# Seven products for the odd layer's key blocks and for the second half of its output projection

## The chip, the core and the metric

The kernel runs on one core of a Trainium2 chip. The metric is the device time of one execution in microseconds (us), as the median of several runs. Durations and waits come from one further execution, taken with the hardware profiler. The engines are PE (TensorE, matmul), DVE (VectorE), ACT (ScalarE), POOL (GpSimd) and SP (SyncE), whose queue issues the weight loads here.

## What is computed

A two-layer trunk on 256 tokens of width 1024, all in float32. Layer 0 mixes tokens by a recurrent branch and sparse attention, layer 1 (the "odd" layer) by retention; after each mixer come a mixture of 32 experts (each token uses 2, every expert's weights are read) and a gated per-layer embedding. The change touches only two products of the odd layer: the key part of `od_w_in` and the projection by `od_w_out`.

```python
def reference(...):
    h = x
    for i in range(DEPTH):                                   # DEPTH = 2
        hn = rms_norm(h, mix_norm_g[i])
        ...
        else:                                                # odd layer
            z = hn @ od_w_in[j]                              # 1024 -> q 1024, k 1024, v 2048, g 2048
            q, k, v, g = _split(z, OD_SPLIT)
            yc = retention_mixer(q..., k..., v..., g, od_gn_g[j])   # 8 heads, rotary q and k
            mix = yc @ od_w_out[j]                           # 2048 -> 1024
        h = h + mix
        h = h + hier_moe(rms_norm(h, ffn_norm_g[i]), ...)    # 32 experts, 1024 -> 512 -> 1024
        e = rms_norm(p[i] @ ple_w_up[i], ple_norm_g[i])
        h = h + e * jax.nn.sigmoid(h @ ple_w_gate[i])
    return h
```

## The kernel before

**Order of the work.** The program is written out by hand, engine by engine; each engine runs its own list in order and semaphores join them. `pe_jobs` lists PE's jobs in order, `banks_of` gives each job one of 8 PSUM banks. `begin` waits until the bank's previous job was emptied, `end` signals "full"; on the other side `full` waits for a job and `emptied`/`taken` free its bank. The tokens' rows are two tiles of 128 (`NT` = 2), `xT` holds the normalised activations turned, features on partitions.

**The odd mixer.** The 1024-wide input meets 12 weight blocks of 1024 x 512 (2 MB each, `rq0`, `rq1`, `rk0`, `rk1`, `rv0..3`, `rg0..3`), then four blocks of the output projection (`rout0..3`, 512 x 1024 each). Query and key blocks go through `tokens` (L629): 8 matmuls of 128x512 for each token tile. DVE then rotates the result (L1774 to L1778), POOL adds the two halves (L1965), PE turns the sum (`turn_rotated`) and ACT copies it out (L1115).

**Seven products.** The four value blocks use the Winograd form of Strassen's scheme. `quarters` cuts a weight block into four quarters of 512 x 256 (B11, B12, B21, B22), `A11..A22` are the quarters of the activations (tile by half of the features). `value_products` (L1038) makes seven products of 4 matmuls of 128x256 (`PRODUCTS`: a, c, b, d, a2, b2, c2) in place of the sixteen matmuls of 128x512. DVE makes the four sums of activations once (`value_sums`, S1 to S4) and four differences of quarters for each block (T3, T1, T2, T4; T1 is written over B12 in the block's slot), one block ahead of PE. ACT copies a, c, b and a2 out, DVE adds the rest together into `rv`.

**The head loop** (`HEAD_STEPS` = 12 steps) runs the 8 heads, the gate blocks and the turned rows `yT0..3`. The output block `rout0` comes in its step 10, `rout1` behind it, then a small product `gain1`, then `rout2` and `rout3`; all go through `held_rows` (L657) into four banks that stay open until `rout3` is done. A 2 MB output block costs 16 matmuls of 128x512. Then DVE adds the banks to `h` (`add_rows`, L1355), with the norm of the first tile in between, and the expert layer `moe(1)` begins: turned rows, routing (L802), the first expert (L874).

**Weights.** Ten slots of 2 MB in `big`: slots 0 to 5 are a ring for the plain blocks; slots 6 to 9 are the `arena`, which holds the mixer's data. SP's queue issues the loads in order and waits before each until its slot is free. For layer 1, experts 0 to 2 take the slots of `EXPERT_SLOTS[1]` in the order gate, up, down: [4, 5, 9], [8, 7, 0], [1, 2, 3]. Slot 9 and those behind it wait for `yT3_1` (`arena_free`), slots 0 to 3 for the reading of `rout0..3`, slot 6 (`SPARE`, a gate of expert 3) for `rout_11`. Half of expert 3's up weights then go into `h` (`lent`) as soon as ACT has copied `h` into PSUM, and later loads wait for an expert to be done.

## Time and profile before

| what | value |
|---|---|
| runs, median (lowest to highest) | 1362.29 us (1360.82 to 1363.45) |
| the profiled execution, its own time | 1363.1 us |
| its span by the trace | 1361.3 us |
| PE busy | 1076.7 us, 79% |
| DVE busy | 355.0 us, 26% |
| DMA queue of the weights | 470.32 MB, 83.7% of 16 engines' span |
| chain that ended last | DMA 48%, PE 46%, DVE 2%, issue 2% |

The busy shares are means over stages with different limits. What counts for a change in one stage is the chain that ended last: for every stretch of time it names the work that the end waited for. A product of a float32 matmul stands in the trace as two records, so 16 matmuls are "x32". The time of an execution is 1.8 us above its span.

### The profile page before, as it was taken

The page shows a single profiled execution, that of the slowest core. Times are in us where ns is not written, and L with a number is a line of the kernel's source. Part 1 is how long each engine was busy: PE and PEld are TensorE (multiplying, and loading weights), DVE is VectorE, ACT ScalarE, POOL GpSimd, SP SyncE. Part 2 cuts the span into 40 slices and gives each one's busy share as a digit, 9 for nine tenths or more (in the row PEclk, how much of TensorE's full clock was granted, in tenths as well). Part 3 has the DMA queues.
Part 4 walks back from the last instruction along what each step waited for, and adds up shares of the span by engine and source line. Part 5 has one row for each costly group of instructions (what it writes and reads, how often), then busy time and mean ns, then how long its engine had stood idle before and what let it go on. Part 6 is the DMA issues. An engine that isn't in the chain of part 4 may idle for free.

```text
span 1361.3 us, 26143 instructions
## 1 busy us (share of the span) xinstructions
PE 1076.7 (79%) x10938; PEld 628.9 (46%) x10938; DVE 355.0 (26%) x826; ACT 170.5 (13%) x411; POOL 90.7 (7%) x226
## 2 busy tenths in 40 slices
PE   6999987676676676689999999988767667766668
PEld 5885554343344343344468554444334333333333
DVE  1596323111111112122254541132211211211121
ACT  2225311000000001001011000121000000000000
POOL 0020011000000000000110100011000000000000
PEclk9999999888888888899999999999888888888889
DMA  9956599999999999998354236789999999999991
GB/s 361 325 197 257 222 403 425 428 430 427 429 429 427 429 428 428 430 407 328 126 183 147 101 124 254 297 345 425 429 428 428 428 428 429 428 428 429 428 416 40
DMA packets 57838, 474.86 MB, mean 349 GB/s; under 512 B 4056, under 2 KB 6104, under 8 KB 32192
## 3 DMA queue, kind: packets, MB, share of 16 engines
q1 hardware_dynamic: 56800, 470.32, 83.7%
q10 hardware_dynamic: 768, 2.57, 0.5%
q0 software_dynamic: 224, 1.31, 0.3%
q8 instruction: 34, 0.56, 0.2%
q14 instruction: 12, 0.10, 0.0%
HBM read 473.12 MB, written 3.16 MB: 350 GB/s over the span
## 4 chain that ended last, share of the span: by engine, by line
DMA 48%; PE 46%; DVE 2%; issue 2%; ACT 1%; SPq 1%; POOL 0%; ACTq 0%; DVEq 0%; POOLq 0%
DMA big<-in_moe_w_up_dram 48%; PE ps L657 10%; PE ps L874 9%; PE ps L629 9%; PE ps L620 5%; PE ps L1038 4%; PE ps L610 1%; PE ps L896 1%; PE ps L785 1%; PE ps L904 1%; SPq L494 1%; PE ps L802 1%; DVE big L1639 0%; DMA h<-in_x_dram 0%; DVE big L1635 0%
## 5 line engine op out<-in xcount | busy, mean ns | idle before, releaser
L874 PE MATMUL ps<-big 128*32 128x256 f32 x4064 | 323.7, 486 | 157.4 <-DMA big<-in_moe_w_up_dram 157.1
L874 PEld LDWEIGHTS ps<-big 128*32 128x32 f32 x4064 | 167.7, 138 | 308.1 <-issue 179.5
L1635 DVE SCALAR_TENSOR_TENSOR big<-big,ps 64x256 f32<-64x256 f32 x64 | 26.4, 413 | 681.3 <-ACT big L1259 681.3
L896 PE MATMUL ps<-big 128*32 128x256 f32 x2048 | 123.8, 382 | 57.7 <-DVE big L1644 57.7
L629 PE MATMUL ps<-big,xT 128*128 128x512 f32 x288 | 125.9, 593 | 2.1 <-DVE xT L1344 1.3
L896 PEld LDWEIGHTS ps<-big 128*32 128x32 f32 x2048 | 59.9, 109 | 108.0 <-DVE big L1644 74.9
L904 PE MATMUL ps<-big 32*128 32x256 f32 x1024 | 73.3, 398 | 41.8 <-ACT big L1270 40.6
L1259 ACT ACTIVATE big<-ps 64x256 f32<-64x256 f32 x64 | 24.1, 377 | 565.9 <-PE ps L874 565.9
L629 PEld LDWEIGHTS ps<-big,xT 128*128 128x128 f32 x288 | 54.3, 190 | 66.2 <-issue 64.3
L904 PEld LDWEIGHTS ps<-big 32*128 32x128 f32 x1024 | 49.5, 184 | 70.8 <-issue 70.8
L657 PE MATMUL ps<-big,xT 128*128 128x512 f32 x160 | 71.8, 607 | 1.5 <-ACT xT L1115 1.5
L620 PE MATMUL ps<-xT,big 128*128 128x256 f32 x320 | 69.9, 380 | 1.5 <-ACT xT L1121 1.5
L1911 POOL TENSOR_TENSOR big<-big,rk 128x64 f32<-128x64 f32 x64 | 18.8, 294 | 773.2 <-PE ps L883 743.8
L657 PE MATMUL ps<-big 128*128 128x512 f32 x160 | 69.5, 593 | 0.0
L844 PE MATMUL ps<-xn,big 128*32 128x256 f32 x1056 | 69.3, 379 | 0.0
L620 PEld LDWEIGHTS ps<-xT,big 128*128 128x128 f32 x320 | 60.6, 190 | 11.7 <-issue 3.7
L657 PEld LDWEIGHTS ps<-big,xT 128*128 128x128 f32 x160 | 30.7, 195 | 39.0 <-issue 36.9
L657 PEld LDWEIGHTS ps<-big 128*128 128x128 f32 x160 | 30.1, 190 | 37.1 <-issue 37.1
L844 PEld LDWEIGHTS ps<-xn,big 128*32 128x32 f32 x1056 | 35.0, 110 | 23.0 <-DVE rk L1597 1.5
L1270 ACT ACTIVATE big<-ps 128x256 f32<-128x256 f32 x64 | 24.5, 383 | 157.0 <-PE ps L896 157.0
L883 PE MATMUL ps<-kept,big 128*32 128x128 f32 x1024 | 40.3, 273 | 0.3 <-issue 0.3
L1639 DVE SCALAR_TENSOR_TENSOR big<-big,ps 64x128 f32<-64x128 f32 x128 | 37.2, 291 | 3.0
(211 smaller groups left out, 805.2 us busy)
## 6 DMA issues: line engine op xcount, KB each, us to landing
big<-in_moe_w_gate_dram SPq DMA_DIRECT2D x64, 2048.0 KB, 33.0
big<-in_moe_w_down_dram SPq DMA_DIRECT2D x62, 2048.0 KB, 38.8
big<-in_moe_w_up_dram SPq DMA_DIRECT2D x60, 2048.0 KB, 37.5
big<-in_od_w_in_dram SPq DMA_DIRECT2D x12, 2048.0 KB, 14.3
big<-in_ev_w_in_dram SPq DMA_DIRECT2D x6, 2048.0 KB, 21.5
big<-in_ple_w_gate_dram SPq DMA_DIRECT2D x8, 1024.0 KB, 20.1
big<-in_od_w_out_dram SPq DMA_DIRECT2D x4, 2048.0 KB, 7.8
big<-in_moe_w_up_dram SPq DMA_DIRECT2D x6, 1024.0 KB, 35.1
```

Of the source, the lines that this page charges most:

```text
L620: ins = nc.tensor.matmul(b[:, i * S:(i + 1) * S], w[:, k, m * P:(m + 1) * P], rhs[:, k, :], start=k == 0, stop=k == KD - 1)
L629: ins = nc.tensor.matmul(b, xT[:, k, t * P:(t + 1) * P], w[:, k, :], start=k == 0, stop=k == KD - 1)
L657: ins = nc.tensor.matmul(banks[job], lhs(k, t), w[:, kk, half * 512:(half + 1) * 512], start=k == 0, stop=k == kt - 1)
L844: ins = nc.tensor.matmul(ps[TOK * q:TOK * q + TOK, 4, 0:QD], pick[:, t, :], xn_t[:, t, q * QD:(q + 1) * QD], start=t == 0, stop=t == NT - 1)
L874: ins = nc.tensor.matmul(ps[TOK * i:TOK * i + TOK, 5, 0:2 * P].rearrange("p (b n) -> p b n", b=2), xe[:, k, :], (low if k < KD // 2 else w ...
L883: ins = nc.tensor.matmul(ps[TOK * q:TOK * q + TOK, 6, t * P:(t + 1) * P], share[:, t, :], ident, start=True, stop=True)
L896: ins = nc.tensor.matmul(ps[TOK * q:TOK * q + TOK, 7, 0:QD], hidT[:, k, :], wd[:, k, q * QD:(q + 1) * QD], start=k == 0, stop=k == KF - 1)
L904: ins = nc.tensor.matmul(ps[:, q, t * QD:(t + 1) * QD], shareT[TOK * q:TOK * q + TOK, t * P:(t + 1) * P], yb[TOK * q:TOK * q + TOK, :], st ...
L1038: ins = nc.tensor.matmul(b, lhs[:, k, :], rhs[:, k, :], start=k == 0 and len(i) == 1, stop=k == HALF - 1, skip_group_check=True)
L1270: sc.activation(yb, ps[:, 7, 0:QD], ACT.Copy).then_inc(y_taken, by)
L1635: ve.scalar_tensor_tensor(out=t2, in0=t2, scalar=1.0, in1=u2, op0=ALU.add, op1=ALU.mult).then_inc(gated_done, by)
L1639: ins = ve.scalar_tensor_tensor(out=hid[2 * TOK * b:2 * TOK * b + 2 * TOK].rearrange("p m k -> p (m k)"), in0=th[0:2 * TOK, b, :], scalar= ...
```

## The change

It turns the two key blocks and the last two output blocks into seven products each.

1. `SEVEN` = rk0, rk1, rv0..3: `products(m)` takes the place of `tokens` for the key blocks and of `value_products`. Six blocks are handled alike, block m in banks 4 to 7 (m even) or 0 to 3 (m odd); `turn_rotated(m + 1)` follows block m for m < 3, in banks 5 and 7 or 1 and 3. DVE now makes the activations' sums and the first block's differences behind the second query tile, ahead of the other two rotations. A key block's results go to `rkraw` in SBUF, and DVE rotates them from there.
2. rout2 and rout3 together are one product of 256 x 1024 by 1024 x 1024, done as seven products of 4 matmuls of 128x512: `last_a`, `last_b`, `last_d`, `last_c` in banks of their own, and three that go on in the banks `rout_00`, `rout_01`, `rout_10`. DVE makes three differences of 128x2048 in step 10 of the head loop and the fourth behind `last_b`, four sums of `yT2` and `yT3` behind the head loop, and adds the parts to `h`.
3. The differences OT2 and OT3 lie in slot 7. So expert 1 gets slots [8, 0, 1] and expert 2 [7, 2, 3], and SP waits for `last_c` and all four differences before slot 7, for `rout_10` before slots 2 and 3, and for `out_parts_used` too before slot 6. `gate1_0` takes slot 7 for slot 1.

```diff
-EXPERT_SLOTS = [[[2, 3, 4], [5, 9, 8], [0, 7, 1]], [[4, 5, 9], [8, 7, 0], [1, 2, 3]]]
+EXPERT_SLOTS = [[[2, 3, 4], [5, 9, 8], [0, 7, 1]], [[4, 5, 9], [8, 0, 1], [7, 2, 3]]]
...
+SEVEN = ("rk0", "rk1", "rv0", "rv1", "rv2", "rv3")
+LAST_BANKS = {"last_b": "yT3_0", "last_d": "yT3_1", "last_c": "gain1"}
...
-    jobs += [f"rv0_{i}" for i in PRODUCTS] + [f"rk1T_{t}" for t in range(NT)]
-    jobs += [f"rv{c}_{i}" for c in range(1, 4) for i in PRODUCTS]
+    jobs += [f"rq0T_{t}" for t in range(NT)]
+    for m, w in enumerate(SEVEN):
+        jobs += [f"{w}_{i}" for i in PRODUCTS] + ([f"{ROTATED[m + 1]}T_{t}" for t in range(NT)] if m < 3 else [])
...
-    jobs += ["gain1"]
+    jobs += ["gain1"] + [f"last_{i}" for i in "abdc"]
...
+                        elif i == RING + 1:
+                            sync.wait_ge(out_tiles_ready, 4)
+                            full(sync, "last_c")
                         expert(l, kind, e, e)
                 if l:
-                    full(sync, "rout_11")
+                    full(sync, "rout_10")
+                    sync.wait_ge(out_parts_used, 1)
...
-            turn_rotated(0)
-            for i, w in enumerate(ROTATED[2:], 1):
-                tokens([f"{w}_{t}" for t in range(NT)], slot(arrived(w), KD, BLK))
-                turn_rotated(i)
...
+            turn_rotated(0)
             pe.wait_ge(sums_ready, 4)
-            value_products(0)
-            turn_rotated(3)
-            for c in range(1, 4):
-                value_products(c)
+            for m in range(len(SEVEN)):
+                products(m)
+                if m < 3:
+                    turn_rotated(m + 1)
...
             gain_rows(1)
-            out_block(2)
-            out_block(3)
...
+            out_product("last_a", OA11, B11)
+            pe.wait_ge(block_read, BLOCK_READ["rout1"])
+            pe.sem_inc(bank_full[BANK["rout_11"]], 1)
+            pe.wait_ge(out_sums_ready, 4)
+            pe.wait_ge(out_tiles_ready, 3)
+            out_product("last_b", OS1, OT1)
+            out_product("last_d", OS2, OT2)
+            out_product("last_c", OS3, OT3)
+            out_product("rout_00", OA12, B21, False)
+            out_product("rout_01", OS4, B22, False)
+            pe.wait_ge(out_tiles_ready, 4)
+            out_product("rout_10", OA22, OT4, False)
             moe(1)
...
+                if m < 2:
+                    for i in ("a2", "b2", "c2"):
+                        taken(dve, f"{w}_{i}")
+                    dve.wait_ge(values_ready, m + 1)
                     for t in range(NT):
+                        rotate(4 + 2 * m + t, rkraw[:, t, :], v)
+                        v.sync()
                         dve.sem_inc(rot_parts, 1)
...
+                if hd == NH + GATE_LAG:
+                    for c in (2, 3):
+                        dve.wait_ge(landed[loads.at[f"rout{c}"]], 16 * loads.turn[f"rout{c}"])
+                    ve.tensor_tensor(OT3, B22, B12, ALU.subtract).then_inc(out_tiles_ready, 1)
+                    ve.tensor_tensor(B12, B12, B11, ALU.subtract).then_inc(out_tiles_ready, 1)
+                    dve.wait_ge(out_tiles_ready, 2)
+                    ve.tensor_tensor(OT2, B22, B12, ALU.subtract).then_inc(out_tiles_ready, 1)
...
+            full(dve, "last_b")
+            ve.tensor_tensor(B12, B21, OT2, ALU.subtract).then_inc(out_tiles_ready, 1)
```

**How the rows stand, at the key blocks.** In the lists below a line number is that of the version shown, "x7" counts matmuls (one record of the list is one matmul, two in the trace), and the semaphores waited for stand in brackets. On PE before, the second key block (bank 1, then 2), the turned key rows (banks 3 and 4) and the first product of `rv0` (bank 4):

```order
L629 MATMUL ps<-big,xT 128x512 [waits bank_free1,landed3]
L629 MATMUL ps<-big,xT 128x512 x7
L629 MATMUL ps<-big,xT 128x512 [waits bank_free2]
L629 MATMUL ps<-big,xT 128x512 x7
L610 MATMUL ps<-kept,big 128x128 [waits bank_free3,rot_ready]
L610 MATMUL ps<-kept,big 128x128 x3
L610 MATMUL ps<-kept,big 128x128 [waits bank_free4,rot_ready]
L610 MATMUL ps<-kept,big 128x128 x3
L1038 MATMUL ps<-big,xT 128x256 [waits bank_free4,landed4,sums_ready]
```

And now, the last three products of the second key block, the turned rows of the first (banks 5 and 7), and the first product of `rv0`:

```order
L1056 MATMUL ps<-big,xT 128x256 [waits bank_free0]
L1056 MATMUL ps<-big,xT 128x256 x3
L1056 MATMUL ps<-big 128x256 [waits bank_free1]
L1056 MATMUL ps<-big 128x256 x3
L1056 MATMUL ps<-big,xT 128x256 [waits tiles_ready,bank_free2]
L1056 MATMUL ps<-big,xT 128x256 x3
L632 MATMUL ps<-kept,big 128x128 [waits bank_free5,rot_ready]
L632 MATMUL ps<-kept,big 128x128 x3
L632 MATMUL ps<-kept,big 128x128 [waits bank_free7,rot_ready]
L632 MATMUL ps<-kept,big 128x128 x3
L1056 MATMUL ps<-big,xT 128x256 [waits bank_free4,landed4]
```

The two runs of 8 matmuls per key block became seven runs of 4 half as wide (four of them stand ahead of the piece), and the bank that `rv0` opens with is no longer one that turned rows have just filled.

On DVE before, from the second difference of `rv0` through the rotation of the second key block to the third difference of `rv1`:

```order
L1748 TENSOR_TENSOR big<-big 128x4x256
L1754 TENSOR_TENSOR big<-big 128x1024 [waits tiles_ready]
L1760 TENSOR_TENSOR big<-big 128x1024 [waits tiles_ready]
L1774 TENSOR_TENSOR xn<-ps,big 128x512 [waits rot_ready,bank_full1]
L1777 TENSOR_TENSOR xn<-ps,big 128x4x64
L1778 TENSOR_TENSOR xn<-ps,big 128x4x64
L1774 TENSOR_TENSOR xn<-ps,big 128x512 [waits bank_free1,rot_ready,bank_full2]
L1777 TENSOR_TENSOR xn<-ps,big 128x4x64
L1778 TENSOR_TENSOR xn<-ps,big 128x4x64
L1743 TENSOR_TENSOR big<-big 128x1024 [waits bank_free2,landed5,bank_full6]
```

And now, from the last additions of `rk0` through its rotation to the first difference of `rv0`:

```order
L1855 TENSOR_TENSOR big<-big,ps 128x256 [waits bank_full6]
L1808 TENSOR_TENSOR big<-big 128x1024 [waits tiles_ready]
L1819 TENSOR_TENSOR xn<-big 128x512 [waits values_ready,bank_free6,rot_ready,bank_free5,bank_free4]
L1821 TENSOR_TENSOR xn<-big 128x4x64
L1822 TENSOR_TENSOR xn<-big 128x4x64
L1819 TENSOR_TENSOR xn<-big 128x512 [waits dve_step,rot_ready]
L1821 TENSOR_TENSOR xn<-big 128x4x64
L1822 TENSOR_TENSOR xn<-big 128x4x64
L1791 TENSOR_TENSOR big<-big 128x1024 [waits dve_step,landed4,bank_full2]
L1796 TENSOR_TENSOR big<-big 128x4x256
```

The rotation of a key block now stands behind the block's last additions and the next block's T4, reads SBUF in place of PSUM, and the differences for the block after next queue behind it.

**At the output projection.** On PE before, `rout1`, `gain1`, `rout2`, `rout3`, and the first turned rows of the expert layer:

```order
L657 MATMUL ps<-big 128x512 x15
L671 MATMUL ps<-xn,kept 32x256 [waits dgain_ready,bank_free1]
L671 MATMUL ps<-xn,kept 32x256 x3
L657 MATMUL ps<-big 128x512 [waits landed2,bank_free2,bank_free0]
L657 MATMUL ps<-big 128x512 x15
L657 MATMUL ps<-big 128x512 [waits landed3,bank_free0,bank_free7]
L657 MATMUL ps<-big 128x512 x15
L610 MATMUL ps<-kept,xn 128x128 [waits xn_ready,landed10,bank_free4,pT_loaded,route_loaded]
L610 MATMUL ps<-kept,xn 128x128 x3
L610 MATMUL ps<-kept,xn 128x128 [waits bank_free6]
```

And now, from `last_a`:

```order
L1118 MATMUL ps<-big 128x512 [waits bank_free6,bank_free5,landed3,landed2,bank_free0]
L1118 MATMUL ps<-big 128x512 x3
L1118 MATMUL ps<-big,xT 128x512 [waits block_read,bank_free5,out_tiles_ready,out_sums_ready]
L1118 MATMUL ps<-big,xT 128x512 x3
L1118 MATMUL ps<-big,xT 128x512 [waits bank_free6]
L1118 MATMUL ps<-big,xT 128x512 x3
L1118 MATMUL ps<-big,xT 128x512 [waits bank_free7]
L1118 MATMUL ps<-big,xT 128x512 x3
L1118 MATMUL ps<-big 128x512 x4
L1118 MATMUL ps<-big,xT 128x512 x4
L1118 MATMUL ps<-big 128x512 [waits out_tiles_ready]
L1118 MATMUL ps<-big 128x512 x3
L632 MATMUL ps<-kept,xn 128x128 [waits xn_ready,landed10,bank_free4,pT_loaded,route_loaded]
```

Two runs of 16 became seven of 4; the first is free to start at once, the second waits for sums and differences from DVE, the seventh for the fourth difference.

On SP before, from expert 0's down weights (slot 9) to those of expert 2 (slot 3), and the gate of expert 3 (slot 6):

```order
L494 DMA big<-in_moe_w_down_dram 128x4096
L494 DMA big<-in_moe_w_gate_dram 128x4096
L494 DMA big<-in_moe_w_up_dram 128x4096
L494 DMA big<-in_moe_w_down_dram 128x4096 [waits block_read]
L494 DMA big<-in_moe_w_gate_dram 128x4096 [waits block_read]
L494 DMA big<-in_moe_w_up_dram 128x4096 [waits block_read]
L494 DMA big<-in_moe_w_down_dram 128x4096 [waits bank_full6]
L548 DMA big<-in_moe_w_gate_dram 128x4096 [waits bank_full6]
```

And now:

```order
L512 DMA big<-in_moe_w_up_dram 128x4096 [waits block_read]
L512 DMA big<-in_moe_w_down_dram 128x4096 [waits block_read]
L512 DMA big<-in_moe_w_gate_dram 128x4096 [waits bank_full7,out_tiles_ready]
L512 DMA big<-in_moe_w_up_dram 128x4096 [waits bank_full3]
L512 DMA big<-in_moe_w_down_dram 128x4096 [waits bank_full3]
L570 DMA big<-in_moe_w_gate_dram 128x4096 [waits out_parts_used,bank_full3]
```

Slots 0 and 1 moved ahead of slot 7; slot 7 now waits for `last_c` and the differences, slots 2 and 3 both for `rout_10`.

## Rows read from the trace of the kernel before

**Rows 1.** the page, the span in 40 slices of 34.03 us
```profile
PEclk9999999888888888899999999999888888888889
GB/s 361 325 197 257 222 403 425 428 430 427 429 429 427 429 428 428 430 407 328 126 183 147 101 124 254 297 345 425 429 428 428 428 428 429 428 428 429 428 416 40
```

**Rows 2.** the chain that ended last, in order of time: start, us, what
```profile
665.41 13.74 PE ps L629 x32
...
694.23 1.09 ACT big L1115 x2
695.46 12.32 PE ps L1038 x56
...
708.66 36.28 PE ps L1038 x168
...
848.50 27.68 PE ps L657 x64
...
921.25 3.63 PE ps L874 x64
...
935.54 26.22 DMA big<-in_moe_w_up_dram
961.81 5.21 PE ps L874 x64
```

**Rows 3.** busy time by stretch, with granted clock, DMA share, GB/s
```profile
core 0: us, PE busy (x) PEld busy (x) DVE busy (x) ACT busy (x) POOL busy (x), PEclk, DMA share, GB/s
600.00:960.00 360.00, 341.43 (x1971) 194.03 (x1970) 123.00 (x270) 42.90 (x100) 28.26 (x47) 1.00 0.63 243
...
834.00:862.00 28.00, 28.00 (x74) 12.24 (x73) 2.67 (x4) 0.00 (x0) 0.00 (x0) 1.00 0.97 403
...
876.00:892.00 16.00, 15.13 (x92) 9.10 (x90) 6.84 (x30) 9.25 (x24) 0.55 (x1) 1.00 0.65 262
892.00:900.00 8.00, 6.95 (x126) 3.91 (x128) 3.60 (x14) 1.96 (x5) 1.92 (x6) 1.00 0.88 298
900.00:936.00 36.00, 30.37 (x552) 17.81 (x544) 10.81 (x27) 4.39 (x12) 3.77 (x10) 1.00 1.01 430
1000.00:1318.00 318.00, 214.74 (x3151) 118.36 (x3140) 48.75 (x130) 25.10 (x66) 19.32 (x61) 0.86 1.01 428
```

**Rows 4.** timeline of PE: start, us, what [idle before <-releaser]
```profile
695.46 1.96 PE L1038 MATMUL ps<-big,xT 128*128 128x256 f32 x8 [0.83 <-ACT big L1115]
```

**Rows 5.** timeline of DVE, key and value blocks
```profile
672.32 0.69 DVE L1774 TENSOR_TENSOR xn<-ps,big 128x512 f32<-128x512 f32 x1 [6.39 <-PE ps L629]
672.93 0.41 DVE L1777 TENSOR_TENSOR xn<-ps,big 128x256 f32<-128x256 f32 x1
...
680.69 0.87 DVE L1732 TENSOR_TENSOR big<-xT 128x512 f32<-128x512 f32 x1
681.48 1.75 DVE L1733 TENSOR_TENSOR big<-xT 128x512 f32<-128x512 f32 x1
...
699.19 1.23 DVE L1743 TENSOR_TENSOR big<-big 128x1024 f32<-128x1024 f32 x1 [4.04 <-PE ps L1038]
```

**Rows 6.** timeline of POOL, the rotated halves' sums
```profile
659.20 1.27 POOL L1965 TENSOR_TENSOR big<-xn 128x512 f32<-128x512 f32 x1 [6.96 <-DVEq L1781]
...
679.73 2.95 POOL L1965 TENSOR_TENSOR big<-xn 128x512 f32<-128x512 f32 x2 [12.11 <-PE ps L610]
```

**Rows 7.** timeline of DVE, end of the head loop
```profile
833.80 1.29 DVE L1813 TENSOR_TENSOR big<-ps,kept 128x512 f32<-128x512 f32 x2 [11.72 <-PE ps L610]
```

**Rows 8.** timeline of SP, weights of the second expert layer
```profile
891.31 0.33 SPq L550 DMA_DIRECT2D h<-in_moe_w_up_dram  x1
```

**Rows 9.** timeline of DVE, after the output projection
```profile
869.42 0.69 DVE L1355 TENSOR_TENSOR h<-h,ps 128x512 f32<-128x512 f32 x1 [2.82 <-PE ps L657]
...
872.19 0.75 DVE L1338 TENSOR_SCALAR xn<-h,nrm 128x1024 f32<-128x1024 f32 x1 [0.66 <-POOL nrm L1884]
```

**Rows 10.** timeline of PE, after the output projection
```profile
877.02 0.66 PE L610 MATMUL ps<-kept,xn 128*128 128x128 f32 x4 [0.42 <-DVE h L1355]
```

More of the change, by code:

```diff
@@ L166, in banks_of @@
             b = fixed[name]
+        elif name in LAST_BANKS:
+            b = bank[LAST_BANKS[name]]
         elif name.startswith(("probT", "pv", "gain0")):
@@ L291, in trunk, with out_quarters @@
         T2, T3, T4 = (view(ro_start + 1024 * i, HALF, VD) for i in range(3))
-        kept_products = [[view(ro_start + 3072 + VD * i, VD) for i in range(4)], [view(4096 + VD * i, VD) for i in range(4)]]
+        kept_products = [[view((5120 + BLK if m == 1 else 4096 if m % 2 else ro_start + 3072) + VD * i, VD) for i in range(4)]
+                         for m in range(len(SEVEN))]
+        rkraw = view(5120 + NH * VD + BLK, NT, 512)
+        def out_quarters():
+            return [held(loads.at[f"rout{2 + i}"], HALF, D)[:, :, BLK * j:BLK * j + BLK] for i in range(2) for j in range(2)]
+        OS1, OS2, OS3, OS4 = (xT2[:, BLK * i:BLK * i + BLK].rearrange("p (k s) -> p k s", k=HALF) for i in range(4))
+        OT2, OT3 = (view(SLOT + HALF * BLK * i, HALF, BLK) for i in range(2))
+        OP1, OP5, OP7, OU2 = (view(o1, BLK) for o1 in (0, BLK, 4 * BLK, 5 * BLK))
+        OA11, OA21, OA12, OA22 = (yT[2 + i][:, :, t * P:(t + 1) * P] for i in range(2) for t in range(NT))
         S1, S2, S3 = (view(17024 + 512 * i, HALF, P) for i in range(3))
@@ L1087, in _, with out_product @@
             gain_rows(1)
-            out_block(2)
-            out_block(3)
+            for c in (2, 3):
+                for t in range(NT):
+                    taken(pe, f"yT{c}_{t}")
+                arrived(f"rout{c}")
+            B11, OT1, B21, B22 = out_quarters()
+            OT4 = OT1
+            def out_product(job, lhs, rhs, fresh=True):
+                b = begin(job) if fresh else bank(job)
+                for k in range(HALF):
+                    ins = nc.tensor.matmul(b, lhs[:, k, :], rhs[:, k, :], start=k == 0 and fresh, stop=k == HALF - 1,
+                                           skip_group_check=True)
+                end(job, ins)
+            out_product("last_a", OA11, B11)
[10 more added lines that the diff above has]
+            out_product("rout_10", OA22, OT4, False)
             moe(1)
@@ L1323, in _ @@
                 sc.activation(rota[:, n % 2, 0, :], bank(name), ACT.Tanh, scale=0.5).then_inc(gtanh_ready, 1)
+            for i, dst in (("a", OP1), ("b", OP5), ("c", OP7)):
+                copy_out(f"last_{i}", dst, bank(f"last_{i}"))
             moe(1)
@@ L1810, in odd_back @@
+            B11, B12, B21, B22 = out_quarters()
             def odd_back(c, t):
@@ L1866, in _ @@
                     odd_back(n // 2, n % 2)
-            gain_diagonals(1)
-            add_rows("rout", 3)
+            for c in (2, 3):
+                for t in range(NT):
+                    taken(dve, f"yT{c}_{t}")
+            ve.tensor_tensor(OS1, OA21, OA22, ALU.add).then_inc(out_sums_ready, 1)
+            ve.tensor_tensor(OS3, OA11, OA21, ALU.subtract).then_inc(out_sums_ready, 1)
+            dve.wait_ge(out_sums_ready, 2)
+            ve.tensor_tensor(OS2, OS1, OA11, ALU.subtract).then_inc(out_sums_ready, 1)
+            dve.wait_ge(out_sums_ready, 3)
+            ve.tensor_tensor(OS4, OA12, OS2, ALU.subtract).then_inc(out_sums_ready, 1)
+            gain_diagonals(1)
+            h11, h12, h21, h22 = (h[:, t, half * 512:(half + 1) * 512] for t in range(NT) for half in range(2))
+            taken(dve, "last_a")
+            v(ve.tensor_tensor(h11, h11, OP1, ALU.add))
+            full(dve, "last_b")
+            ve.tensor_tensor(B12, B21, OT2, ALU.subtract).then_inc(out_tiles_ready, 1)
+            full(dve, "last_d")
+            emptied("last_d", ve.tensor_tensor(OU2, OP1, bank("last_d"), ALU.add))
+            taken(dve, "last_b")
+            taken(dve, "last_d")
+            v(ve.tensor_tensor(OP5, OU2, OP5, ALU.add))
+            v(ve.tensor_tensor(h21, h21, OU2, ALU.add))
+            v.sync()
+            v(ve.tensor_tensor(h12, h12, OP5, ALU.add))
+            taken(dve, "last_c")
+            v(ve.tensor_tensor(h21, h21, OP7, ALU.add))
+            v(ve.tensor_tensor(OP5, OP5, OP7, ALU.add))
+            v.sync()
+            full(dve, "rout_11")
+            dve.wait_ge(block_read, BLOCK_READ["rout1"])
+            ve.tensor_tensor(h22, h22, OP5, ALU.add).then_inc(out_parts_used, 1)
+            dve.wait_ge(out_parts_used, 1)
+            emptied("rout_11", ve.tensor_tensor(h22, h22, bank("rout_11"), ALU.add))
+            for job, part in (("rout_00", h11), ("rout_01", h12), ("rout_10", h21)):
+                full(dve, job)
+                emptied(job, ve.tensor_tensor(part, part, bank(job), ALU.add))
+                taken(dve, job)
+                if job == "rout_01":
+                    dve.sem_inc(h_ready, 1)
+                    normalise(3, 0)
+            taken(dve, "rout_11")
+            dve.sem_inc(h_ready, 1)
             moe(1)
```

179 lines of the change are left out of this document (91 added, 88 removed).

## The prediction

> **What bounds the kernel now.** I read four views, in this order. First the page's slices [rows 1]: from the 18th to the 27th of them (about 612 to 918 us) the DMA rate falls to 101 to 345 GB/s, while on both sides it stands at 428 to 430. So the odd layer's mixer and the start of its experts are not bound by loads, and the long stretches beside them are. Second the chain in order of time [rows 2]: from 665 us to 935 us it is nearly all PE, the key block of 13.74 us, the value blocks, the two last output blocks of 27.68 us, the first experts. At 935.54 a load of expert weights takes over, and then loads carry the chain to the end. Third the stretches [rows 3]: DMA is idle 35% of 876 to 892 and 12% of 892 to 900, and full from 900 on (1.01, 430 GB/s), though PE is on the chain until 935. What PE saves ahead of 900 moves the moment from which loads are full; the bytes behind it take as long as before. So a microsecond less of PE ahead of 900 is a microsecond less at the end, as long as the idle time of DMA there is enough for what has to be loaded. Last the timelines, for what hides beside PE.
>
> **The change, part by part.**
>
> *Key blocks.* A key block is 32 records of 128x512, 13.74 us. A value block is 56 records of 128x256, and three of them take 36.28 us, 12.09 us each [rows 2]. The new key blocks are the same instructions on the same kinds of operands, so 13.74 - 12.09 = 1.65 us each, 3.30 us for two. The first value block took 12.32 us; were the key blocks as long, it would be 2.84 us. I take 12.09, from three blocks against one, and the first block of the row keeps its extra 0.23 whichever it is.
>
> *A wait that goes.* Before, the first product of `rv0` uses bank 4, which the turned key rows have just filled, and PE waits 0.83 us for ACT to empty it [rows 4]. In the new order turned rows lie in banks 5 and 7 or 1 and 3, and the next block opens with another bank (4 or 0) and a third (6 or 2); it comes to the first of the shared banks after two products, 2 x 12.09/7 = 3.5 us. ACT's two copies take 1.09 us [rows 2]. So the 0.83 us go and nothing takes their place: 4.13 us for this part.
>
> *What DVE must do for it.* The sums and the first differences now come behind the second query tile, which PE ends at least 6.9 us ahead of the first key block (a tile of the other query block, half of 13.74 us, lies between): a rotation of 0.69 + 0.41 + 0.41 = 1.5 us, sums of 0.87 + 1.75 and two more near 0.69, then four differences of 1.23 [rows 5]. That is 1.5 + 4.0 + 4.9 = 10.4 us in a row, but the first product needs only rotation and sums (5.5 us of the 6.9), and each later one finds its difference 1.2 us after the last while PE takes 1.7 us a product. The other two rotations follow, 3 us, and PE wants their sum only a block later. For a key block DVE then has four differences (4.9 us), five additions of 128x256 (2.1 us) and two rotations (3.0 us): 10.0 us in a PE time of 12.09 and the turning. It is late at the start of the next block, by about the 3 us of the rotations, but differences are made a block ahead, so PE doesn't see it. I cost it at nothing; the cover is that lead of 9 us or so. If it were gone, the price is at most the two pairs of rotations, 6 us.
>
> POOL's additions are the second load. Alone one takes 1.27 us, two that met DVE's sums took 2.95, and one of these sums took 1.75 us where its neighbour of the same shape took 0.87 [rows 5, 6]. So where both work out of SBUF one stretches the other by up to the length of the other's instruction. The rotation of a key block now reads SBUF alone and meets POOL's addition: at worst 2 x 1.27 us more per key block, 12.6 us for DVE. That is still about PE's time, and is what rival C rests on. The Trainium skill ("SBUF — State Buffer", Who interferes with whom) says that a DVE instruction with two SBUF inputs and a GpSimd instruction that reads SBUF block each other, one for the whole length of the other; the 1.75 us agree with it. By that rule the rotations become instructions that can be blocked, where those reading PSUM could not.
>
> *Output projection.* Two blocks are 64 records of 128x512 in 27.68 us [rows 2], 0.4325 us each. Seven products of 4 matmuls are 56 such records, 24.22 us: 3.46 us saved. Waits: `last_a` needs nothing new. `last_b` needs three differences of 128x2048 and four sums. A difference of 1024 columns takes 1.23 us and a sum of 512 takes 0.69 to 0.87 [rows 5]; by that slope 2048 columns take some 2.3 us (an estimate), three of them 6.9 us. They stand in step 10 of the head loop, where DVE is idle for 11.72 us ahead of the copies of `yT3` [rows 7]: hidden, with 4.8 us to spare. Were the cover gone, the rest would delay `yT3` and PE with it; from both sides it is 0 to 2 us. The sums (about 3 us) come behind `yT3`, while PE has the 14 us of `rout1`. The fourth difference starts at the end of `last_b` and has five products, 17 us. The additions of parts, nine or ten of 0.69 us, fit in the same 17 us beside it.
>
> *The end of the projection.* Before, the second tile's last bank is emptied 0.69 us after PE's end and PE waits 0.42 us for it in the turned rows [rows 10]; the bank that it needs then is free early now. But the first tile's norm has less cover. It takes from the add at 869.42 to 872.19 + 0.75 = 872.94, 3.5 us [rows 9]; behind `rout_01` there were 6.9 us of products, and now there is one, 3.46 us. So PE waits about 0.1 us in place of 0.42. Behind it the second tile's norm starts as long after PE's end as before, and routing hangs on that. Of the 0.3 I count 0.1; bounds: 0.5 us lost to 0.4 gained.
>
> *Loads.* Slot 7 is now filled when `last_c` is done: four products, 13.8 us behind `gain1`, the time at which slot 2 was filled before. Slots 2, 3 and 6 all wait for the last product, where before it was 3 and 6. So 2.1 MB more are left at PE's end, 4.9 us at 430 GB/s. DMA's idle time between 876 and 900 is 0.35 x 16 + 0.12 x 8 = 6.6 us [rows 3]. It takes them, with 1.7 us over. The half of expert 3 that goes into `h` is issued 15.1 us behind PE's end [rows 8]; three loads take 14.6 us, so it is hardly held up. Cost nothing, bounds 0 to 3.5 us (all that the projection saves).
>
> *Sum.* 3.30 + 0.83 + 3.46 + 0.1 = 7.7 us. The profiled execution took 1363.1 us, 1.8 above its span of 1361.3, and 0.8 above the median of the runs. 1363.1 - 7.7 = 1355.4 for it, and 1362.3 - 7.7 = 1354.6 as median.
>
> **The rivals.**
>
> A, the forecast: all of it arrives. 1354.6, give or take 1.3 for the runs and 0.5 for the terms.
>
> B, the loads left at PE's end outlast the idle time. For it: 4.9 of 6.6 us are used, and each load needs a while before its first bytes. Against it: DMA must only be full again when expert 0 frees its slots. It would give back a part of the projection's 3.5 us: 1354.6 to 1358.1.
>
> C, DVE is late at the key blocks and PE waits for a difference. For it: 12.6 us of work at worst for PE's 12.1 and the turning. Against it: the lead of a block. 1 to 6 us back: 1355.6 to 1360.6.
>
> D, the time is fixed by loads earlier than I read, and PE's gain is idle time: 1361 to 1363. Against it: 101 to 183 GB/s in five slices of the mixer [rows 1], under half of the 430 that the queue can do.
>
> E, slower. PE's granted clock is 1.00 over 600 to 960 and 0.86 over 1000 to 1318 [rows 3], the two levels being 2.4 and 1.2 GHz; the same 64 records take 3.63 us in the one stretch and 5.21 in the other [rows 2], 1.44 times as long. If the new small waits, or narrow products in a row, let the clock fall there, the six blocks of 72.5 us would become 104, and the time 1386. It decides from 7.7 + 2.7 = 10.4 us lost, that is 24 us of PE work at the lower rate. Against it: the four value blocks are such products already, with a wait of 0.83 us ahead, at 1.00; in the slower stretch PE stood still a third of the time (214.74 us busy of 318) behind loads. The place where it could happen is the stretch from the first key block to `gain1`.
>
> That the change doesn't do what it says I leave out: the lists of rows show the 28 matmuls of half width for a key block and 28 for the two output blocks.
>
> **How the numbers follow.** A 0.79, B 0.09, C 0.05, D 0.03, E 0.04. The likeliest is A, 1354.6. The range of eight in ten is A with the runs' spread below and most of B above: 1352.8 to 1357.8. A measurement of this kernel can tell 0.2% (2.7 us) from no change. Faster by more than that: A, B and most of C, 0.91. Within it: the rest of C and D, 0.05. Slower: E, 0.04.
>
> **What would show it right or wrong.** In the profile of the changed kernel: two more groups of 56 records of 12.1 us ahead of the value blocks; no wait of 0.83 us at the first product of `rv0`; 56 records in 24.2 us for the last part of the projection, with no gap at its second and seventh product; DVE's three long differences inside the gap of 11.7 us, at 2.3 us each; PE's wait behind the projection below 0.3 us; DMA nearly without a hole from the end of the projection, and full some 7.7 us earlier than at 900; the change of hands from PE to loads near 928. It is wrong if PE waits for a difference in a key block (C), if full DMA comes less early than the end of the projection did (B), if the span behind the change of hands is longer (D), or if the granted clock falls below 1.00 ahead of 950 (E).

## The result

| kernel | median | lowest to highest | runs |
|---|---|---|---|
| before | 1363.38 us | 1360.82 to 1368.01 | 8 |
| changed | 1356.85 us | 1355.77 to 1359.69 | 8 |

The ratio is 0.9949, with a 95% interval of 0.9937 to 0.9961: 7.0 us faster (5.3 to 8.6). The two medians of the table lie 6.5 us apart; from here on gains are given by the ratio, which has the interval. On another chip the same kernel came to 0.9947 (0.9934 to 0.9960), 7.2 us. Forecast were 7.7 us and 1354.6 us. The forecast stood on a median of 1362.29 us from three runs; the eight runs beside the changed kernel put it at 1363.38.

The profiled execution of the changed kernel took 1359.69 us, with a span of 1357.9. So its span is only 3.4 us shorter than that of before, and it is the slowest of its eight. Of the 3 to 4 us that are missing there, 3.0 are explained in the last section; the place of the change itself is read from times relative to a mark ahead of it.

**The slices** of the changed kernel's page answer to [rows 1]:

```profile
PEclk9999999888888888889999999999888888888889
GB/s 361 327 194 259 223 401 425 429 429 429 428 429 428 430 428 430 428 410 330 139 179 145 110 124 239 284 393 427 427 428 429 428 429 428 430 428 429 429 413 38
```

The rates are as before, and the dip lies in the same slices.

**The chain in order of time** (start, us, what) answers to [rows 2]:

```profile
668.55 12.09 PE ps L1056 x56
...
681.52 12.09 PE ps L1056 x56
...
694.48 12.09 PE ps L1056 x56
...
707.44 36.28 PE ps L1056 x168
...
847.28 20.81 PE ps L1118 x48
...
930.91 27.99 DMA big<-in_moe_w_up_dram
```

The two key blocks are 56 records of 12.09 us, where one was 32 records of 13.74; the block behind them takes 12.09 and not 12.32, with no wait ahead; the three after it are the same 36.28 us, for which the chain has one piece. Of the seven products of the projection six stand as one piece, 48 records in 20.81 us, and the seventh behind it. Then loads take over at 930.91 (before: 935.54); the forecast was near 928.

**Busy time by stretch** (PE, PEld, DVE, ACT, POOL busy, then granted clock, DMA share, GB/s) answers to [rows 3]:

```profile
871.50:887.40 15.90, 14.99 (x92) 9.18 (x91) 6.97 (x31) 9.25 (x24) 0.55 (x1) 1.00 0.95 386
887.40:895.40 8.00, 6.95 (x127) 3.92 (x128) 3.59 (x13) 1.96 (x5) 1.92 (x6) 1.00 0.88 295
895.40:931.30 35.90, 30.34 (x552) 17.81 (x544) 10.73 (x27) 4.32 (x12) 3.77 (x10) 1.00 1.01 425
```

Behind the projection DMA is busy 95% of the stretch where it was 65%, 88% in the next as before, and then full.

**Against a mark.** The first product of the second query tile is the last piece of PE's work that the change leaves alone. From its start (650.57 before, 653.71 after) to the issue by which SP answers the release of the arena (834.23, 833.01) are 183.66 and 179.30 us; from there to the load into `h` 57.08 and 53.67 us; from there to the landing that ends PE's first wait for loads 70.4 and 72.2 us. The issues in the timeline of SP (start, us, what), of the kernel before and then the changed one:

```profile
834.23 0.38 SPq L487 DMA_DIRECT2D big<-in_ple_w_up_dram  x1
```

```profile
833.01 0.38 SPq L505 DMA_DIRECT2D big<-in_ple_w_up_dram  x1
...
886.68 0.33 SPq L572 DMA_DIRECT2D h<-in_moe_w_up_dram  x1
```

The first two differences are PE's: 4.36 + 3.41 = 7.8 us. The same three times for the kernels of this and the next section, from their own profiles (those that load DVE or change POOL are told further down):

| kernel | mark to arena release | to the load into `h` | to the landing | sum |
|---|---|---|---|---|
| before | 183.66 | 57.1 | 70.4 | 311.2 |
| before, again | 183.66 | 57.1 | 71.6 | 312.3 |
| changed | 179.30 | 53.7 | 72.2 | 305.2 |
| changed, again | 179.30 | 53.7 | 71.8 | 304.8 |
| keys only | 179.30 | 57.4 | 71.9 | 308.6 |
| projection only | 183.66 | 53.7 | 72.1 | 309.4 |
| slot 7 late | 179.30 | 53.7 | 76.0 | 309.0 |
| slot 3 early | 179.30 | 53.7 | 72.3 | 305.3 |
| slot 3 early, values by head | 178.20 | 53.7 | 72.0 | 303.9 |
| slot 3 early, values by head, again | 178.20 | 53.7 | 70.7 | 302.6 |
| one product more | 179.30 | 57.1 | 72.8 | 309.2 |

The first two columns repeat within 0.01 to 0.05 us wherever the program is the same. The third varies by 1.1 us between the two profiles of before and by 1.3 us between the last kernel's two. What comes behind the landing is the same for old and new kernels, within its own spread: 399.5 and 397.3 us to the end of the span before, 399.0 and 397.2 us in the changed kernel, 397.1 to 400.3 us over all 14 profiles. So from the mark to the end are 710.7 and 709.6 us before, 704.2 and 702.0 us changed.

### The profile page after: what moved, and what is told of

It reads as the page before. It is cut to its first block, busy times and chain, and to the rows that moved or that the text cites. A ratio compares the mean times of both kernels' runs of the same rounds, so it can differ in the third digit from the quotient of the medians.

```text
span 1357.9 us, 26296 instructions
## 1 busy us (share of the span) xinstructions
PE 1071.7 (79%) x10978; PEld 636.9 (47%) x10978; DVE 389.8 (29%) x860; ACT 175.4 (13%) x422; POOL 90.3 (7%) x226
## 4 chain that ended last, share of the span: by engine, by line
DMA 48%; PE 46%; DVE 2%; issue 2%; ACT 1%; SPq 1%; POOL 0%; DVEq 0%; ACTq 0%; POOLq 0%
DMA big<-in_moe_w_up_dram 48%; PE ps L896 10%; PE ps L679 8%; PE ps L651 7%; PE ps L1056 5%; PE ps L642 5%; PE ps L1118 2%; PE ps L632 2%; PE ps L918 1%; PE ps L807 1%; PE ps L926 1%; SPq L512 1%; PE ps L824 1%; DVE big L1687 0%; DMA h<-in_x_dram 0%
## 5 line engine op out<-in xcount | busy, mean ns | idle before, releaser
L651 PE MATMUL ps<-big,xT 128*128 128x512 f32 x224 | 98.1, 593 | 2.1 <-DVE xT L1392 1.3
L926 PEld LDWEIGHTS ps<-big 32*128 32x128 f32 x1024 | 49.5, 184 | 70.7 <-issue 70.7
L679 PE MATMUL ps<-big,xT 128*128 128x512 f32 x160 | 73.8, 620 | 1.5 <-ACT xT L1159 1.5
L651 PEld LDWEIGHTS ps<-big,xT 128*128 128x128 f32 x224 | 42.4, 190 | 51.8 <-issue 49.9
L679 PEld LDWEIGHTS ps<-big,xT 128*128 128x128 f32 x160 | 31.3, 199 | 40.3 <-issue 38.3
L1056 PE MATMUL ps<-big 128*128 128x256 f32 x192 | 43.4, 379 | 0.0
L679 PE MATMUL ps<-big 128*128 128x512 f32 x96 | 41.8, 593 | 0.0
L1056 PEld LDWEIGHTS ps<-big 128*128 128x128 f32 x192 | 36.5, 190 | 4.9
```

The source lines that it names most:

```text
L651: ins = nc.tensor.matmul(b, xT[:, k, t * P:(t + 1) * P], w[:, k, :], start=k == 0, stop=k == KD - 1)
L679: ins = nc.tensor.matmul(banks[job], lhs(k, t), w[:, kk, half * 512:(half + 1) * 512], start=k == 0, stop=k == kt - 1)
L926: ins = nc.tensor.matmul(ps[:, q, t * QD:(t + 1) * QD], shareT[TOK * q:TOK * q + TOK, t * P:(t + 1) * P], yb[TOK * q:TOK * q + TOK, :], st ...
L1056: ins = nc.tensor.matmul(b, lhs[:, k, :], rhs[:, k, :], start=k == 0 and len(i) == 1, stop=k == HALF - 1, skip_group_check=True)
```

## The experiments

**The two halves.** The changed kernel again, and each part alone.

```diff
 keys only: the key part as changed, and in the projection
-            for c in (2, 3): ... the seven products
+            out_block(2)
+            out_block(3)
 projection only: the projection part as changed, and for the key blocks
-            for m in range(len(SEVEN)): products(m) ...
+                tokens([f"{w}_{t}" for t in range(NT)], slot(arrived(w), KD, BLK))
+                turn_rotated(i)
```

> The changed kernel again, beside its two halves on one chip. Theory: the sum of the two halves, less what the loads give back: 6.0 to 7.7 us under the kernel before. In the profile the projection ends 7.8 us earlier relative to the second query tile's first product, and a load takes over from PE near 930 us. Rival (loads hold nothing back): 7.7 us under, and the takeover by loads as much earlier as the projection's end.

Measured: 0.9947 (0.9934 to 0.9960), 7.2 us under the kernel before (5.5 to 9.0), which holds the theory's 6.0 to 7.7 and the rival's 7.7 alike. The profile has the load taking over at 930.24, and PE's part is 7.8 us, as expected.

> Only the key blocks as seven products; the output projection, its slots and its waits as before. Theory: PE's 4.1 to 4.4 us all arrive, since no load is moved behind the projection: 4.1 us under the kernel before. Rival: loads hold back a part of whatever PE saves: 3.3 us or less under.

Measured: 0.9971 (0.9959 to 0.9983), 4.0 us (2.3 to 5.6): the theory's 4.1, but the rival's 3.3 lies inside as well. PE's part by the table is 4.36 less 0.34, which it loses behind the projection; the timeline of PE (start, us, what, idle time before it) names the wait:

```profile
875.82 1.06 PE L628 MATMUL ps<-kept,xn 128*128 128x128 f32 x8 [0.94 <-DVE h L1372]
```

0.94 us for DVE's last addition, where it was 0.42 [rows 10]. Banks are dealt in turn to the jobs that have no fixed one. The key products have fixed banks, so fewer jobs are dealt, and `rout_11` falls into bank 4, which the first turned rows need; before, it was bank 6, that of the second ones.

> Only the last two output blocks as seven products, with their slots and waits; the key blocks as before. Theory: PE's end of the projection comes 3.45 us earlier, but one more load of 2.1 MB is left at that point and 1 to 1.8 us are given back: 1.7 to 2.5 us under the kernel before. Rival (loads hold nothing back): 3.4 us under.

Measured: 0.9988 (0.9977 to 0.9999), 1.6 us (0.1 to 3.1). The interval holds the theory's 1.7 to 2.5 and leaves the rival's 3.4 just outside, but the profile doesn't bear out the theory's reason: the third column has 72.1 us, where the keys-only kernel, which leaves one load fewer behind, has 71.9. Why the whole runs show less than PE's 3.4 us stays open. The halves sum to 5.6 us, the whole is 7.2; each has an interval of 1.5 to 1.8 us either way, so the sum says nothing against the whole.

**Loads left at the projection's end.** Was anything given back there?

```diff
 slot 7 late
                             sync.wait_ge(out_tiles_ready, 4)
-                            full(sync, "last_c")
+                            full(sync, "rout_10")
 slot 3 early
-EXPERT_SLOTS = ... [7, 2, 3]]]
+EXPERT_SLOTS = ... [7, 3, 2]]]
-("gate1_1", 2)
+("gate1_1", 3)
-"rout3": "rout_10"
+"rout3": "rout_01"
```

> The changed kernel, but the load into slot 7 waits for the last product (rout_10) as those into slots 2, 3 and 6 do: four loads, 8.4 MB, left at the projection's end in place of three. Theory: DMA's idle time behind the projection is used up (some 1.4 us left), so of the 4.9 us that this load takes 3.5 to 4.9 come on top: 3.5 to 4.9 us above the changed kernel, DMA busy without a hole from the projection's end. Rival (PE alone sets the end there): as the changed kernel within 1 us.

Measured: 0.9972 (0.9959 to 0.9984), 3.4 us above the changed kernel beside it. SP's queue shows the four issues at one point:

```profile
869.55 0.33 SPq L512 DMA_DIRECT2D big<-in_moe_w_gate_dram  x1
869.92 0.43 SPq L512 DMA_DIRECT2D big<-in_moe_w_up_dram  x1
870.40 0.43 SPq L512 DMA_DIRECT2D big<-in_moe_w_down_dram  x1
870.93 1.32 SPq L570 DMA_DIRECT2D big<-in_moe_w_gate_dram  x1
```

and the table the price: 76.0 us in the third column in place of 72, 4.0 us. One such load takes 4.9 us at 430 GB/s. So of DMA's idle time behind the projection about 1 us could still be used. By its shares of 95% and 88% the changed kernel has 0.8 + 1.0 us idle there, and this version, in the same two stretches from the projection's end, has not lost all of it:

```profile
869.50:885.40 15.90, 15.02 (x91) 9.18 (x91) 6.92 (x31) 9.25 (x24) 0.55 (x1) 1.00 0.94 385
885.40:893.40 8.00, 6.95 (x129) 3.92 (x128) 3.58 (x13) 1.96 (x5) 1.92 (x6) 1.00 0.97 411
```

At 94% and 97% some 1.2 us stay idle. The theory had DMA without a hole here; that much was wrong.

> The changed kernel, but expert 2's up weights take slot 3 and its down weights slot 2, and slot 3 is released by rout_01, one product (3.46 us) before the end of the projection, since rout3 is read last by the product b2. So two loads are left at the end in place of three, as before. Theory (the load left behind costs 1 to 1.8 us): 1 to 1.8 us under the changed kernel, 8 to 9 us under the kernel before; in the profile 303.1 to 304.0 us from the second query tile to the landing near 957, where the changed kernel had 304.8 and 305.2. Rival (what was given back has another cause): as the changed kernel.

Measured: 0.9931 (0.9912 to 0.9951); the changed kernel's 0.9947 lies inside. The trace speaks against a gain: SP issues the load at 867.86, 3.4 us ahead of the next at 871.30, and the landing comes 305.3 us behind the mark, where the changed kernel had 305.2 and 304.8. My theory was wrong here: the third load is hidden, and leaving it behind costs nothing that these times can show.

> The kernel before, profiled once more, to see how much of a profile's time from the second query tile (its first product) to the landing that ends PE's wait near 960 us is the execution's own. It was 311.2 us in the first profile. Theory: within 0.5 us of that, so that the 308.7 us of the keys-only kernel mean that 1.8 us of PE's 4.4 were given back by the loads. Rival: 312 us or more, the first profile being the odd one, and the keys-only kernel gave nothing back.

Measured: 312.3 us, of which 71.6 in the third column, against 70.4 in the first profile. So the rival holds (312 us or more): the profile that I had compared with was early by 1.1 us, and what the loads seemed to give back (1.8 us, from 70.4 to 72.2) is 0.2 to 0.6 us against this one. Whether that rest is real can't be told from executions that differ by more: the version with the values by head has 72.0 us in one profile and 70.7 in the other.

> The changed kernel with one product of 4 matmuls of 128x512 done twice ahead of last_a, which adds 8 records, 3.46 us, to PE alone. Theory: on the path, but part of it falls into the time that DMA needs anyway behind the projection: 1.7 to 3.5 us above the changed kernel. Rival (loads set the end from the projection on): under 1 us above.

Measured: 0.9979 (0.9963 to 0.9995), against 0.9947 to 0.9949 some 4.2 us above the changed kernel, with 3.45 us in the second column. That is above the theory's range; with both intervals it is 4.2 give or take some 2.8 us, so whether a part of it is hidden can't be told. The rival's 1 us is ruled out: PE sets the end at the projection, and the trace puts all 3.45 us ahead of the load into `h`.

**DVE's cover at the key blocks.** Extra differences that change nothing, each of 128x1024. This version and the two after it have one execution each, so they are read by their traces:

```diff
+                if m < 2:
+                    for _ in range(4):          # 8 in the second version
+                        v.sync()
+                        v(ve.tensor_tensor(T4, quarters(m + 1)[2], T2, ALU.subtract))
+                    v.sync()
                 if m < len(SEVEN) - 1:
                     fourth_tile(m + 1)
```

> The changed kernel with DVE loaded by four more differences of 128x1024 (4.9 us) behind each of the two key blocks' last additions, ahead of the fourth difference and the rotation. Theory (differences are made a block ahead, PE needs the next at 7.7 us behind DVE's making of it): PE waits nowhere in the six blocks, 179.3 us from the second query tile's first product to the release of the arena as in the changed kernel. Rival (DVE and PE are about even in the key blocks, 12.6 against 13.0 us): PE waits for most of the 9.8 us.

Measured: 181.81 us from the mark to the arena's release, 2.5 more than the theory's 179.3, and far less than the rival's 9.8. PE waits at one place, and not for a difference. Its timeline at the turned rows of the second key block:

```profile
705.49 0.66 PE L632 MATMUL ps<-kept,big 128*128 128x128 f32 x4
708.10 0.66 PE L632 MATMUL ps<-kept,big 128*128 128x128 f32 x4 [1.96 <-POOL big L2075]
```

1.96 us for POOL's second sum of the rotated halves. In the changed kernel that sum ends at 699.23 + 1.26 = 700.5 us

```profile
699.23 1.26 POOL L2070 TENSOR_TENSOR big<-xn 128x512 f32<-128x512 f32 x1 [1.36 <-DVEq L1865]
```

and PE comes to it at 706.57 + 0.43 = 707.0. So the cover is 6.5 us, and its end is the turned rows, not the next block's differences as I had held. At its second rotation of a key block DVE was 5.0 us late after the first block (unseen by PE) and 8.7 after the second.

> As the last one with eight more differences per key block, 9.8 us each. Theory: now DVE is behind by more than the cover of 7.7 us, and PE waits some 2 to 6 us after the first key block and again after the second, 5 to 12 us in all. Rival (the cover is a whole block or more on each): below 3 us.

Measured: 12.6 us more from the mark to the arena's release (191.92 us). Waits of PE, summed (us, times, longest), name both chains:

```profile
PE ps L1056 <- DVE big L1808: 4.4, 2, 3.8
PE ps L632 <- POOL big L2075: 4.0, 3, 2.0
```

A fourth difference, wanted by the last product of the block, is late too. These waits are 8.4 of the 12.6 us; what the rest waits for this list doesn't say. The block `rv0` starts 3.9 us later behind the mark than in the changed kernel, `rv1` 12.4, so the second key block costs 8.6 us, above the 2 to 6 expected for each, and the whole is a little above the theory's 5 to 12.

**Who stretches DVE.** In the changed kernel DVE's timeline at a rotation and the first difference behind it:

```profile
672.49 0.69 DVE L1819 TENSOR_TENSOR xn<-ps,big 128x512 f32<-128x512 f32 x1 [0.22 <-DVE xn L1822]
...
674.06 2.26 DVE L1791 TENSOR_TENSOR big<-big 128x1024 f32<-128x1024 f32 x1 [0.22 <-DVE xn L1822]
...
682.15 0.69 DVE L1819 TENSOR_TENSOR xn<-big 128x512 f32<-128x512 f32 x1
...
683.66 1.80 DVE L1819 TENSOR_TENSOR xn<-big 128x512 f32<-128x512 f32 x1
...
686.35 2.27 DVE L1791 TENSOR_TENSOR big<-big 128x1024 f32<-128x1024 f32 x1 [0.22 <-DVE xn L1822]
```

and POOL's beside it:

```profile
672.40 1.27 POOL L2070 TENSOR_TENSOR big<-xn 128x512 f32<-128x512 f32 x1 [8.80 <-DVEq L1830]
683.65 1.26 POOL L2070 TENSOR_TENSOR big<-xn 128x512 f32<-128x512 f32 x1 [8.40 <-DVEq L1865]
686.27 1.27 POOL L2070 TENSOR_TENSOR big<-xn 128x512 f32<-128x512 f32 x1 [1.36 <-DVEq L1865]
```

The same shapes take 0.69 or 1.80 us, and 1.22 (elsewhere) or 2.26, the long ones each beside an addition of POOL; the addition keeps its 1.26 us. The query tile's rotation at 672.49 has POOL beside it too, but reads PSUM (`ps`) and one SBUF operand, and keeps 0.69. The run writes a constant there for the key tiles, so the rotated keys are left out:

```diff
+                if n < 4: po.tensor_tensor(...)
+                else: po.memset(rotd[:, n % 2, :], 0.25).then_inc(rot_ready, 1)
```

> The changed kernel, with POOL's four additions for the key tiles replaced by writing a constant into the same place (the rotated keys are left out, so the output is another). Theory: what stretched DVE's instructions to 1.80 and 2.26 us is POOL's reading of SBUF; they fall back to 0.69 and 1.22 us. Rival: POOL's writing does it, and they stay long. Either way PE's 179.3 us stay.

Measured: DVE, and POOL under it, from one timeline each:

```profile
672.92 2.26 DVE L1791 TENSOR_TENSOR big<-big 128x1024 f32<-128x1024 f32 x1 [0.22 <-DVE xn L1822]
...
682.53 0.69 DVE L1819 TENSOR_TENSOR xn<-big 128x512 f32<-128x512 f32 x1
...
684.11 1.23 DVE L1791 TENSOR_TENSOR big<-big 128x1024 f32<-128x1024 f32 x1 [0.22 <-DVE xn L1822]
```

```profile
672.84 1.26 POOL L2071 TENSOR_TENSOR big<-xn 128x512 f32<-128x512 f32 x1 [0.29 <-DVEq L1830]
682.50 0.53 POOL L2074 MEMSET big<- 128x512 f32 x1 [8.40 <-DVEq L1865]
684.01 0.53 POOL L2074 MEMSET big<- 128x512 f32 x1 [0.98 <-DVEq L1865]
```

Beside the last addition of POOL (672.84) the difference still takes 2.26 us; beside the two writes, 0.69 and 1.23. So it is POOL's reading of SBUF that stretches a DVE instruction with two SBUF inputs, by 1.1 us for an addition of 1.26. The Trainium skill ("SBUF — State Buffer", Who interferes with whom) says that a DVE instruction with two SBUF inputs contends with a GpSimd instruction that reads SBUF, and not with one that only writes it; the runs agree. PE's 179.30 us stay, since the 4 x 1.1 us lie inside the cover of 6.5.

**A wait that the change left.** Ahead of the first head PE waits 0.82 us for the last values:

```profile
741.81 1.89 PE L1056 MATMUL ps<-big,xT 128*128 128x256 f32 x8
744.52 0.67 PE L1086 MATMUL ps<-big 128*128 128x256 f32 x2 [0.82 <-DVE big L1855]
```

The version waits for each value block where a head first reads it, on top of slot 3 early:

```diff
-            for c in range(4): ... taken(pe, f"rv{c}_{i}")
-            pe.wait_ge(values_ready, len(SEVEN))
...
                     pe.wait_ge(inner_ready, g + 1)
+                    if g % 2 == 0:
+                        for i in ("a2", "b2", "c2"):
+                            taken(pe, f"rv{g // 2}_{i}")
+                        pe.wait_ge(values_ready, g // 2 + 3)
```

> As the kernel with slot 3 early, and the wait of 0.82 us at the first head product goes: values are waited for at the second product of each second head, not all before the first. Theory: PE's path saves 0.4 to 0.8 us more, since the first head's product needs no values. Rival: DVE, which still has two additions of the last value block to do, delays the first head's decay by as much: nothing.

> The kernel with slot 3 early and the values waited for head by head once more. In its first profile 178.20 us passed from the second query tile to the release of the arena, 1.10 less than in the changed kernel. Theory: 8 us under the kernel before, 0.992 to 0.995 of it. Rival (loads hide what PE saves): 7 us or less, above 0.995.

Measured: 0.9947 (0.9928 to 0.9966), then 0.9940 (0.9926 to 0.9954), 7.2 and 8.2 us under the kernel before. In the trace the head follows the last product at once

```profile
742.31 1.89 PE L1056 MATMUL ps<-big,xT 128*128 128x256 f32 x8
744.04 0.59 PE L1082 MATMUL ps<-big 128*128 128x256 f32 x2
```

and the mark-to-release time falls by 1.10 us in both profiles, more than the 0.4 to 0.8 expected; the rival is ruled out. The second set's 8.2 us and 0.9940 are what was expected of it, but its interval reaches above the 0.995 of the rival. It is the shortest PE path of all versions run; by the times of whole runs it can't be told from the changed kernel.

## Why the prediction was right

The reading of what bounds the stretch held: what PE saves there, 7.8 us in the trace, arrives at the end, within 1.7 us as far as whole runs can tell. The time fell by 7.0 us for a forecast of 7.7, with 5.3 to 8.6 as interval. The median came out at 1356.85 for 1354.6: 1.1 of these 2.3 us are the base, which three runs had put too low, and 1.2 the difference of the medians, 6.5 for 7.7. Step by step:

*Key blocks and the bank.* Forecast 3.30 + 0.83 = 4.13 us, measured 4.36. The difference is the 0.23 us by which the first value block was longer (12.32): I kept it, and it went with the wait ahead of it, all six blocks being 12.09 now. No difference was late, as held. But the reason that I gave was wrong: the cover is 6.5 us and not 9, and it ends at the turned rows, not at the next block's differences. POOL did stretch DVE, by 1.1 us per addition, inside the worst case of 1.27 that I had set, and stayed at 1.26 itself.

*Projection.* Forecast 3.46 us, measured 3.4. The three long differences took 2.28 and 2.29 us each, for an estimate of 2.3, and left 4.99 us of DVE's gap, for 4.8. For the fourth I had counted five products, 17 us; between `last_b` and `rout_10` are four, 13.8 us. It ran from 854.38 to 856.67, and `rout_10` starts at 868.09, so nothing hung on the slip. DVE's timeline, the three and the copies behind them:

```profile
820.78 2.28 DVE L1926 TENSOR_TENSOR big<-big 128x2048 f32<-128x2048 f32 x1
822.98 2.29 DVE L1927 TENSOR_TENSOR big<-big 128x2048 f32<-128x2048 f32 x1
825.30 2.29 DVE L1929 TENSOR_TENSOR big<-big 128x2048 f32<-128x2048 f32 x1
832.58 1.29 DVE L1872 TENSOR_TENSOR big<-ps,kept 128x512 f32<-128x512 f32 x2 [4.99 <-PE ps L632]
```

*Behind it.* I counted on 0.1 us gained, since PE would wait 0.1 us in place of 0.42. It waits 0.46, above the 0.3 that I had named as the mark of being right:

```profile
864.48 3.60 PE L1118 MATMUL ps<-big,xT 128*128 128x512 f32 x8
867.92 3.60 PE L1118 MATMUL ps<-big 128*128 128x512 f32 x8
871.97 1.06 PE L632 MATMUL ps<-kept,xn 128*128 128x128 f32 x8 [0.46 <-DVE xn L1386]
```

From the last product (starting at 868.09, by 847.28 + 20.81, when `rout_01` is full) to the turned rows are 3.9 us. I had taken the chain from the start of DVE's addition to the end of its norm, 3.5, and left out the handing over at both ends. Nothing was gained or lost by it: from the end of the projection to the first expert are 16.42 us before (876.18 to 892.60) and 16.44 after (871.54 to 887.98).

*Loads.* 6.6 us of idle time for 4.9 us of load, 1.7 over, was right in kind: the third load cost nothing that can be seen, the fourth cost 4.0 us where 4.9 - 1.7 = 3.2 would follow. So the margin was nearer 1 us, since not all of the idle time can be filled. Rival B had its place right, but needs one load more than the change leaves there. The change of hands, forecast near 928, came at 930.91. Behind the mark that is 277.2 us, where the forecast gives 935.54 - 7.7 - 650.57 = 277.3; the difference is that the mark itself came 3.1 us later in this execution.

*The other rivals.* C: no wait of PE in the six blocks; it would have needed more than 6.5 us of lateness. D: refuted by the product more. E: the granted clock is 1.00 from 640 to 950 us, the whole stretch of the change. By the letter of the forecast E's sign, a clock below 1.00 ahead of 950, did appear, at 602 to 610 us, but ahead of the change, and in one of the two profiles of before as well. E's price was also too low: I took 1.44 from a stretch in which both levels are mixed. In the piece that starts at 605.12 in the last section the records of 128x512 start 0.85 us apart at a granted clock of 0.50 and 0.43 at 1.00, twice as long.

## What to carry to other kernels

Where an engine is on the chain and loads idle behind it, count the bytes that the change leaves to be loaded against that idle time; until what can be filled of it is used up, the engine's microseconds are the kernel's. When a bank's reuse makes a wait of 0.4 to 0.9 us, any change in the number of jobs moves it, so read the list of banks with the change. And compare profiles from a mark just ahead of the change, not by their spans.

## What I had not expected

Behind a long stretch bound by loads, PE's clock falls once more in some executions and not in others. Behind layer 0's last expert, the chain in the first profile of before, and then of the changed kernel, at the same instructions:

```profile
602.33 1.11 PE ps L610 x8
604.15 7.11 PE ps L657 x16
```

```profile
602.52 1.88 PE ps L632 x8
605.12 9.28 PE ps L679 x16
```

In the changed kernel's profile the granted clock falls to 0.50, the level of 1.2 GHz, between 602 and 610 us, after it had been 1.00; in that of before it stays at 1.00:

```profile
602.00:604.00 2.00, 1.48 (x8) 1.47 (x8) 0.89 (x2) 0.00 (x0) 0.00 (x0) 0.67 1.03 410
604.00:606.00 2.00, 1.27 (x3) 0.50 (x2) 1.39 (x2) 0.60 (x1) 0.00 (x0) 0.50 1.01 393
...
608.00:610.00 2.00, 2.00 (x5) 0.72 (x4) 0.00 (x0) 0.00 (x0) 0.00 (x0) 0.62 1.05 386
610.00:612.00 2.00, 2.00 (x6) 0.90 (x5) 0.00 (x0) 0.00 (x0) 0.00 (x0) 1.00 1.05 385
```

PE had been busy in both; it reached these rows out of a stretch in which it waited for loads. That makes 3.0 us between the two executions, before the change even begins. Of 14 profiles the mean clock over 600 to 616 us was 1.00 in six, 0.89 in two and 0.79 in six; the two profiles of before fall one into the first and one into the last group, and so do the two of the changed kernel. It is one part of the spread of the times, 3 to 8 us from lowest to highest in each set of runs, and not the whole: the six profiles at 1.00 reach the mark at 650.6 to 653.5 us, and what comes behind the landing varies by 3 us more. How often the clock fell in the runs without a profile isn't known. So parts of 1 us could only be told by the trace.
